# Seven block products for the branch gates of a hybrid layer, and merged sums kept raw until the last unit

## The chip, the cores and the metric

One core of one Trainium2 chip runs the whole network as one program. The metric is the device time of an execution in microseconds (us). TensorE (PE) multiplies matrices into PSUM banks; VectorE (DVE), ScalarE (ACT) and GpSimd (POOL) do the element-wise work; SyncE's queue (SP) issues the loads.

## The reference

A sequence of 512 tokens of width 1024 goes through an FFN, an attention mix, a second FFN, two hybrid layers and a last norm, all in float32. The change touches the end of a hybrid layer, where three branches `a`, `c`, `r` of width 512 are merged under gates that are three of the projections `h @ w_in`:

```python
def hybrid_layer(x, norm_g, w_in, ..., w_branch, w_out, layer):
    h = rms_norm(x, norm_g)
    proj = h @ w_in
    ...
    g = jax.nn.sigmoid(gates.astype(jnp.float32)).reshape(b, s, N_BRANCH, D_MODEL)
    branches = (a, c, r)
    merged = g[:, :, 0] * (branches[0] @ w_branch[0])
    for i in range(1, N_BRANCH):
        merged = merged + g[:, :, i] * (branches[i] @ w_branch[i])
    return x + (merged @ w_out).astype(x.dtype)
```

## The kernel before

**Products in two parts.** Each float32 operand is split into a high part (a rounded copy) and a low part (the rest), and a product is three matmuls, high by high, low by high, high by low (`three`, L1987 to L1989). Activations lie transposed in `xt_hi` and `xt_lo`, 8 blocks of 128 channels by 512 tokens. Weights come as slabs of 512 KB, 1024 float32 per partition: SP loads them in a fixed order into a ring of six slots (`load`, L512), ACT makes the high part (`highs`, L796), POOL the low part (`lows`, L665), PE uses the slab and gives the slot back (`w_used`). ACT casts `LEAD` = 4 slabs ahead of PE.

**The merge of a layer** is 12 units. Unit `nn` is branch `b = nn % 3` of the pair `jj = nn // 3` of output tiles (128 of the 1024 channels each), and takes three slabs: two of gate weights and one of branch weights. PE runs two gate tiles (`feature_tile`, 24 matmuls of 512 columns each) and the branch product (two times 12 of 512). ACT takes the sigmoid of each gate tile from its PSUM bank into `gate_sb` (L1224). DVE multiplies and adds, tile by tile:

```python
if b == 0:
    dve.tensor_tensor(m_sum[:, jh, :], src, g, ALU.mult)                  # L1957
else:
    dve.tensor_tensor(m_tmp[:, :], src, g, ALU.mult)                      # L1959
    ins = dve.tensor_tensor(m_sum[:, jh, :], m_sum[:, jh, :], m_tmp[:, :], ALU.add)   # L1961
```

After the third branch ACT makes the high part of the sum (L1280) and DVE the low (L1971). When all eight merged tiles stand, `out_product` multiplies them by `w_out`, eight more slabs of the same ring. Unit 2 also waits for `br_lo`, the low part of branch `r` (L1862).

**The FFN's seven products.** From its fourth unit on, an FFN takes its gate and up tiles (as one 2 by 2 block matrix) with the Strassen-Winograd scheme: seven products of half-size blocks instead of eight, each 12 matmuls of 256 columns (`product`, L2145 to L2147). That asks for sums of the activation blocks, made once (`x_sums`, their lows L1442), sums of the weight blocks per unit (DVE L1454, L1456, L1458 into PSUM, one by POOL, L729; their highs by ACT, lows by DVE L1463 and POOL L711), and combinations of the products on DVE (L1474 to L1516) and ACT (L938). The first three units run as plain tiles, with L1408 as their last step.

Every engine runs its own instructions in the order in which they are written, so what is queued behind a waiting instruction waits with it.

Of the kernel before, what the change touches and what calls it, by code (L numbers as in the profile page):

```python
# [8 lines left out]
ALU = mybir.AluOpType  # L9
# [6 lines left out]
P = 128  # L16
# [13 lines left out]
F0 = 3  # L30

# [101 lines left out]
def build(nc, x, ffn1_pre_g, ffn1_post_g, ffn1_w_gate, ffn1_w_up, ffn1_w_down, mix_pre_g, mix_post_g,  # L133
# [4 lines left out]
    with ExitStack() as ctx:  # L138
# [119 lines left out]
        m_hi_late = on("m_hi_late", [4, SEQ], 24, F32R)  # L258
# [6 lines left out]
        m_lo_late = on("m_lo_late", [4, SEQ], 48, F32R)  # L265
# [10 lines left out]
        m_lo_early = on("m_lo_early", [4, SEQ], 80, F32R)  # L276
# [92 lines left out]
        hhalf_done = sem("hhalf_done")  # L369
# [134 lines left out]
        def _(sp):  # L504
# [95 lines left out]
            for l in range(LAYERS):  # L600
# [25 lines left out]
                for jj in range(4):  # L626
# [7 lines left out]
                    if jj == 0:  # L634

                        sp.wait_ge(r_a_done, 16 * (l + 1))
                        gain(g_pre, norm_g_2[1:2, :] if l == 0 else final_norm_g_2.rearrange("(o d) -> o d", o=1),
                             pre_in)
                out_loads(s, w_out_2[l])
# [14 lines left out]
        def _(pool):  # L654
# [103 lines left out]
            for l in range(LAYERS):  # L758
# [11 lines left out]
                for h in range(4):  # L770
# [4 lines left out]
                    pool.tensor_tensor(sq_lo[:, :], r_sq[:, :], f32(sq_hi[:, :]), ALU.subtract).then_inc(rql_done, 1)  # L775
            lows(done, N_SLABS)
# [3 lines left out]
        def _(act):  # L780
# [10 lines left out]
            def highs(upto):  # L791

                for s in range(cast[0], min(upto, N_SLABS)):
# [3 lines left out]
                    cast[0] = s + 1  # L797

# [74 lines left out]
            def ffn(n):  # L873
# [18 lines left out]
                def x_sum_high(m):  # L892

                    act.wait_ge(xs_made, 4 * n + (1, 3, 3, 4)[m - 1])
                    act.activation(xs_hi[m][:, :, :], xs_raw[m][:, :, :], ACT.Copy).then_inc(xsh_done, 1)

# [18 lines left out]
                def up_high(s):  # L915

                    i = slot_of[s]
                    wait_raw(act, s)
                    act.activation(hi_slots[i][:, 512:SLAB], raw_slots[i][:, 512:SLAB], ACT.Copy).then_inc(hi_ready, 1)
                    cast[0] = s + 1  # L920

                highs(s0 + 2 * F0)
                gate(0)
                x_sum_high(1)
                x_sum_high(2)
                gate(1)
                x_sum_high(3)
                x_sum_high(4)
# [176 lines left out]
            for l in range(LAYERS):  # L1105
# [111 lines left out]
                def gate(nn, jh):  # L1217

                    n = 12 * l + nn
                    b4 = 4 if nn < 3 else 0  # L1220
# [46 lines left out]
                for nn in range(12):  # L1267
                    for jh in range(2):
                        highs(merge + 3 * nn + jh + 1 + LEAD)
# [5 lines left out]
                    highs(merge + 3 * nn + 3 + LEAD)  # L1275
                    if nn % 3 == 2:
                        for jh in range(2):
                            k = 2 * (nn // 3) + jh
                            act.wait_ge(ms_done, 8 * l + k + 1)
                            act.activation(m_hi(k), m_sum[:, jh, :], ACT.Copy).then_inc(mh_done, 1)  # L1280
# [5 lines left out]
        def _(dve):  # L1286
# [108 lines left out]

            def ffn(n):
# [13 lines left out]

                def quarter(k0, c0):

                    sl = slice(256 * c0, 256 * c0 + 256)
                    return f32(xt_hi[:, 4 * k0:4 * k0 + 4, sl]), f32(xt_lo[:, 4 * k0:4 * k0 + 4, sl])

                def whole(m, k0, c0):

                    hi, lo = quarter(k0, c0)
                    return dve.tensor_tensor(xs_part[m][:, :, :], hi, lo, ALU.add)  # L1419

                def x_sums():

                    dve.wait_ge(xtl_done, 8 * (2 * n + 1))
                    x11, x21, x22, x12 = (xs_part[m][:, :, :] for m in (2, 3, 1, 4))
                    s1, s2, s3, s4 = (xs_raw[m][:, :, :] for m in (1, 2, 3, 4))
                    whole(3, 0, 1)
                    link(whole(1, 1, 1))
                    dve.tensor_tensor(s1, x21, x22, ALU.add).then_inc(xs_made, 1)
                    link(whole(2, 0, 0))
                    dve.wait_ge(xs_made, 4 * n + 1)  # L1430
# [6 lines left out]
                def x_sum_low(m):  # L1437

                    dve.wait_ge(xsh_done, 4 * n + m)
                    if m < 4:  # L1440
                        dve.wait_ge(xs_made, 4 * n + 4)
# [1176 lines left out]
```

## Time and profile before

| what | value |
|---|---|
| median of 3 runs | 2048.14 us (2048.11 to 2048.17) |
| the profiled execution | 2048.16 us, span 2046.4 us |
| granted PE clock over the span | 1.00 |
| PE busy | 2028.4 us, 11280 matmuls |
| chain that ended last | PE 91%, DVE 6%, ACT 2% |
| the merge's PSUM sigmoids, L1224 | 48, mean 598 ns |
| slab loads | 3.4 to 3.9 us from issue to landing |

An engine's busy time counts instructions at work. A matmul's duration in the timeline is longer than the distance to the next one's start, because matmuls are pipelined: what a stretch of PE takes is read from starts.

### The profile page before, as it was taken

How to read it: one execution, taken by the hardware profiler on the slowest of the kernel's cores; microseconds unless marked ns; L12 is line 12 of the kernel's file. 1: busy time of each engine (PE TensorE's matmuls, PEld its weight loads, DVE VectorE, ACT ScalarE, POOL GpSimd, SP SyncE). 2: the span in 40 equal slices, each digit the busy share in tenths (PEclk: the TensorE clock that was granted, in tenths of full speed). 3: DMA queues.
4: the chain of work that ended last, by engine and by line, in shares of the span. 5: the costliest groups of instructions: out<-in, count | busy, mean ns of one | idle time of the engine just before them, and what ended most of it. 6: DMA issues, size and time to landing. Idle time of an engine off the chain costs nothing.

```text
span 2046.4 us, 28715 instructions
## 1 busy us (share of the span) xinstructions
PE 2028.4 (99%) x11280; PEld 1736.5 (85%) x11280; DVE 1110.8 (54%) x1822; ACT 910.1 (44%) x1657; POOL 994.3 (49%) x544
## 2 busy tenths in 40 slices
PE   9999999999999999999999999999999999999998
PEld 8999988877788999988888888888888888888887
DVE  7777720877848777802357674611133677562112
ACT  5445623467754444613444544322243544352222
POOL 4666644246654666643444343544434443364441
PEclk9999999999999999999999999999999999999999
DMA  6333332311133333333322222333333222233332
GB/s 190 99 105 109 104 97 93 122 42 32 32 113 104 104 104 105 102 103 114 108 74 75 73 80 82 103 100 96 93 129 93 72 73 79 76 103 94 94 102 72
DMA packets 244278, 191.53 MB, mean 94 GB/s; under 512 B 6448, under 2 KB 208816, under 8 KB 243760
## 3 DMA queue, kind: packets, MB, share of 16 engines
q1 hardware_dynamic: 244144, 189.70, 30.7%
q8 instruction: 90, 1.47, 0.3%
q14 instruction: 44, 0.36, 0.1%
HBM read 187.58 MB, written 2.10 MB: 93 GB/s over the span
## 4 chain that ended last, share of the span: by engine, by line
PE 91%; DVE 6%; ACT 2%; issue 1%; SPq 0%; DMA 0%; POOL 0%; DVEq 0%; ACTq 0%
PE bank L1987 22%; PE bank L1989 21%; PE bank L1988 21%; PE bank L2145 6%; PE bank L2146 6%; PE bank L2147 6%; PE bank L1981 3%; PE bank L2278 1%; PE bank L2446 1%; PE bank L2298 1%; DVE xs_lo L1442 1%; PE bank L2305 1%; DVE xs_part L1419 1%; DVE xn L1304 0%; DVE x_tok L1309 0%
## 5 line engine op out<-in xcount | busy, mean ns | idle before, releaser
L665 POOL TENSOR_TENSOR w_lo<-w_raw,w_hi 128x1024 fp32r<-128x1024 f32 x248 | 612.8, 2478 | 610.9 <-ACT w_hi L796 609.9
L796 ACT ACTIVATE w_hi<-w_raw 128x1024 fp32r<-128x1024 f32 x287 | 300.8, 1054 | 227.7 <-DMA w_raw<-in_ffn_w_down 125.6
L1987 PE MATMUL bank<-xt_hi,w_hi 128*128 128x512 f32 (+1 forms) x896 | 343.0, 383 | 0.5
L1988 PE MATMUL bank<-xt_lo,w_hi 128*128 128x512 f32 (+1 forms) x896 | 338.9, 378 | 0.0
L1989 PE MATMUL bank<-xt_hi,w_lo 128*128 128x512 f32 (+1 forms) x896 | 338.9, 378 | 0.0
L1987 PEld LDWEIGHTS bank<-xt_hi,w_hi 128*128 128x128 f32 x896 | 168.5, 188 | 39.3 <-issue 6.7
L1989 PEld LDWEIGHTS bank<-xt_hi,w_lo 128*128 128x128 f32 x896 | 168.6, 188 | 32.0
L1988 PEld LDWEIGHTS bank<-xt_lo,w_hi 128*128 128x128 f32 x896 | 168.7, 188 | 29.7
L1987 PE MATMUL bank<-w_hi,xt_hi 128*128 128x512 f32 (+1 forms) x456 | 178.2, 391 | 0.0
L1989 PE MATMUL bank<-w_hi,xt_lo 128*128 128x512 f32 (+1 forms) x456 | 174.4, 383 | 0.0
L1988 PE MATMUL bank<-w_lo,xt_hi 128*128 128x512 f32 (+1 forms) x456 | 174.3, 382 | 0.0
L1987 PE MATMUL bank<-w_hi,h_hi 128*128 128x512 f32 x352 | 137.1, 390 | 0.0
L1988 PE MATMUL bank<-w_lo,h_hi 128*128 128x512 f32 x352 | 137.0, 389 | 0.0
L1989 PE MATMUL bank<-w_hi,h_lo 128*128 128x512 f32 x352 | 136.9, 389 | 0.0
L2145 PE MATMUL bank<-xs_hi,ws_hi 128*128 128x256 f32 x456 | 129.3, 283 | 0.0
L2146 PE MATMUL bank<-xs_lo,ws_hi 128*128 128x256 f32 x456 | 129.0, 283 | 0.0
L2147 PE MATMUL bank<-xs_hi,ws_lo 128*128 128x256 f32 x456 | 129.0, 283 | 0.0
L1959 DVE TENSOR_TENSOR m_tmp<-bank,gate_sb 128x512 f32<-128x512 f32 x32 | 22.1, 692 | 180.2 <-PE bank L1989 179.6
L734 POOL TENSOR_TENSOR w_lo<-w_raw,w_hi 128x1024 fp32r<-128x1024 f32 x38 | 91.8, 2415 | 30.6 <-ACT w_hi L796 19.1
L1224 ACT ACTIVATE gate_sb<-bank 128x512 f32<-128x512 f32 x48 | 28.5, 598 | 173.6 <-PE bank L1989 173.6
L1298 DVE RECIPROCAL stat<-stat 128x1 f32<-128x1 f32 x12 | 2.0, 163 | 190.1 <-ACT stat L808 190.1
L1987 PEld LDWEIGHTS bank<-w_hi,xt_hi 128*128 128x128 f32 x456 | 85.7, 188 | 20.2 <-issue 3.0
(358 smaller groups left out, 4874.2 us busy)
## 6 DMA issues: line engine op xcount, KB each, us to landing
w_raw<-in_w_in SPq DMA_DIRECT2D x132, 512.0 KB, 3.8
w_raw<-in_ffn_w_down SPq DMA_DIRECT2D x44, 512.0 KB, 3.6
w_raw<-in_ffn_w_gate SPq DMA_DIRECT2D x43, 512.0 KB, 3.8
w_raw<-in_ffn_w_up SPq DMA_DIRECT2D x43, 512.0 KB, 3.9
w_raw<-in_w_out SPq DMA_DIRECT2D x24, 512.0 KB, 3.7
w_raw<-in_w_branch SPq DMA_DIRECT2D x24, 512.0 KB, 3.4
w_raw<-in_w_qkv SPq DMA_DIRECT2D x16, 512.0 KB, 3.9
x_tok<-in_x SPq DMA_DIRECT2D x4, 512.0 KB, 7.0
```

Source lines behind the costliest of these rows:

```text
L665: pool.tensor_tensor(lo_slots[i], raw_slots[i], f32(hi_slots[i]), ALU.subtract).then_inc(lo_ready, 1)
L734: pool.tensor_tensor(lo_slots[i], raw_slots[i], f32(hi_slots[i]), ALU.subtract).then_inc(lo_ready, 1)
L796: act.activation(hi_slots[i], raw_slots[i], ACT.Copy).then_inc(hi_ready, 1)
L1224: act.activation(gate_sb[:, jh, :], bank[b4 + jh][:, :], ACT.Sigmoid).then_inc(gs_done, 1)
L1959: dve.tensor_tensor(m_tmp[:, :], src, g, ALU.mult).then_inc(gm_done, 1)
L1981: ins = pe.matmul(dst[:, cols(k)], blk, ident[:, :], is_transpose=True)
L1987: pe.matmul(out_ap, ah, bh, start=first, stop=False)
L1988: pe.matmul(out_ap, ah, bl, start=False, stop=False)
L1989: return pe.matmul(out_ap, al, bh, start=False, stop=last)
L2145: pe.matmul(dst, wh, xh, start=k == 0 and not onto, stop=False, skip_group_check=onto)
L2146: pe.matmul(dst, wh, xl, start=False, stop=False, skip_group_check=onto)
L2147: ins = pe.matmul(dst, wl, xh, start=False, stop=k == 3, skip_group_check=onto)
```

## The change

Units 4 to 11 of both layers (`M0` = 4) no longer compute their two gate tiles with 48 matmuls of 512 columns, but with seven products of 12 matmuls of 256 columns, in the order P1, P6, P4, P2, P7, P5, P3, in banks `g_x`, `g_y`, `g_v`, `g_z`, `g_w`. The activation sums (`ms_*`) are made on DVE and ACT during units 2 to 4 of each layer. The weight sums S3, S2 and S4 (DVE) lie in the PSUM banks of the branch products (`p_a`, `p_b`) and in `g_t`; sum 1 is made by POOL (`t_raw1`, L831, and its low, L842). Combinations v1 (ACT, L1385), v2 and v3 (DVE) give four quarter tiles, with a sigmoid of 256 columns each. The merged sums stay raw in SBUF (`m_raw`), the product with the gate stays in PSUM, and the splits into `m_hi` and `m_lo` come in unit 11. The load of the next norm's gain moves from behind the first pair's slabs to behind the fifth `w_out` slab. Core of the diff:

```diff
+M0 = 4
...
                 out_loads(s, w_out_2[l], next_gain)
...
+                def next_gain():
+                    sp.wait_ge(prod_done, gate_product(l, 11, 4))
+                    gain(g_pre, ..., pre_in)
...
+                for nn in range(M0, 12):                                   # POOL
+                    q, g = before_gate(l, nn), merge_start(l) + 3 * nn
+                    if nn > M0:
+                        lows(g - 1, g)
+                        pool.wait_ge(ws1l_done, q)
+                    pool.tensor_tensor(t_raw1[:, :], raw_slots[j][:, 0:512], raw_slots[i][:, 0:512], ALU.subtract)
+                    pool.wait_ge(ws_made, 3 * q + 3)
+                    pool.tensor_tensor(lo_slots[i], raw_slots[i], f32(hi_slots[i]), ALU.subtract).then_inc(lo_ready, 1)
+                    pool.tensor_tensor(lo_slots[j][:, 512:SLAB], raw_slots[j][:, 512:SLAB], ...)
+                    pool.tensor_tensor(lo, pairs(t_raw1[:, :]), f32(hi), ALU.subtract).then_inc(ws1l_done, 1)
...
+                for nn in range(M0, 12):                                   # ACT
+                    act.activation(v1[:, :], g_x, ACT.Copy).then_inc(u1_done, 1)
+                    highs(g + 3)
+                    if nn < 11:
+                        gate_sum_high(nn + 1, 2)
+                        gate_sum_high(nn + 1, 4)
+                    sigmoid(0, 0, g_x)
+                    if nn < 11:
+                        highs(g + 4)
+                        up_high(g + 4)
+                    else:
+                        for k in range(4):
+                            merged_high(k)
+                    sigmoid(0, 1, g_v)
+                    if nn < 11:
+                        gate_sum_high(nn + 1, 3)
+                        gate_sum_high(nn + 1, 1)
+                    sigmoid(1, 1, g_z)
+                    act.wait_ge(uplo_done, q + 1)
+                    sigmoid(1, 0, g_w)
+                merged_high(4)
+                merged_high(5)
+                highs(merge + N_MERGE + 2)
...
+                        dve.tensor_tensor(src, src, g, ALU.mult).then_inc(gm_done, 1)          # merged, L2089
+                        dve.tensor_tensor(m_raw[k][:, :], src, m_raw[k][:, :], ALU.add)        # L2092
...
+                def gate_w_sums(nn):
+                    dve.tensor_tensor(g_sum[3], w2[:, 512:SLAB], w2[:, 0:512], ALU.subtract)   # L2111
+                    dve.tensor_tensor(g_sum[2], g_sum[3], w1[:, 0:512], ALU.add)               # L2113
+                    dve.tensor_tensor(g_sum[4], g_sum[2], w1[:, 512:SLAB], ALU.subtract)       # L2115
...
+                    merged(nn)                                             # DVE, unit M0 - 1
+                gate_sum_low(M0, 4)
+                x_sum_low(2 + l, 1, 3, ms_hi, ms_lo, ms_raw)
+                gate_sum_low(M0, 3)
+                x_sum_low(2 + l, 4, 4, ms_hi, ms_lo, ms_raw)
+                for nn in range(M0, 12):                                   # DVE
+                    if nn < 11:
+                        gate_w_sums(nn + 1)
+                    dve.tensor_tensor(v2[:, :], g_y, v1[:, :], ALU.add).then_inc(u2_done, 1)   # L2155
+                    if nn < 11:
+                        gate_sum_low(nn + 1, 2)                                                # L2122
+                        gate_sum_low(nn + 1, 4)
+                    dve.tensor_tensor(v3[:, :], g_y, v1[:, :], ALU.add).then_inc(u3_done, 1)
+                    dve.tensor_tensor(g_v, v3[:, :], g_v, ALU.subtract).then_inc(gsum_done, 1)
+                    dve.wait_ge(prod_done, gate_product(l, nn, 5))
+                    dve.tensor_tensor(v2[:, :], g_z, v2[:, :], ALU.add).then_inc(upart_done, 1)  # L2168
+                    dve.tensor_tensor(g_z, g_z, v3[:, :], ALU.add).then_inc(uphi_done, 1)        # L2170
+                    if nn < 11:
+                        gate_sum_low(nn + 1, 3)
+                    else:
+                        for k in range(4):
+                            merged_low(k)
+                    dve.tensor_tensor(g_w, g_w, v2[:, :], ALU.add).then_inc(uplo_done, 1)        # L2178
+                    if nn == 11:
+                        merged_low(4)
+                        merged_low(5)
+                    merged(nn)
...
+                    pe.wait_ge(u2_done, q + 1)                             # PE: P7, then P5, P3
+                    product(g_y, gate_w_sum(3, s), m_sum(3), onto=True).then_inc(prod_done, 1)
+                    pe.wait_ge(ws1l_done, q + 1)
+                    for jh in range(2):
+                        wait_merged(pe, l, nn - 1, jh)
+                    pe.wait_ge(gs_done, gate_count(l, nn - 1, 1) - 1)
+                    product(g_z, gate_w_sum(1, s), m_sum(1)).then_inc(prod_done, 1)
+                    ready(s + 1)
+                    product(g_w, w_quarter(s + 1, 1), m_sum(4)).then_inc(w_used, 1)
+                    if nn < 11:
+                        pe.wait_ge(wsl_done, 3 * q + 6)
+                    branch_product(nn, (p_a, p_b))
```

How the order of instructions moves is shown at three places. First DVE's queue in a late unit of the first layer's merge, before: the end of a unit with `b` = 2 and what follows (`m_tmp`, `m_sum` in SBUF, `bank` is a PSUM bank).

```order
L1959 TENSOR_TENSOR m_tmp<-bank,gate_sb 128x512 [waits gs_done,ms_done]
L1961 TENSOR_TENSOR m_sum<-m_sum,m_tmp 128x512 [waits gm_done]
L1971 TENSOR_TENSOR m_lo_late<-m_sum,m_hi_late 128x512 [waits mh_done,ms_done]
L1971 TENSOR_TENSOR m_lo_late<-m_sum,m_hi_late 128x512 [waits mh_done]
L1957 TENSOR_TENSOR m_sum<-bank,gate_sb 128x512 [waits mh_done,ml_done,gs_done,w_used]
L1957 TENSOR_TENSOR m_sum<-bank,gate_sb 128x512 [waits ml_done,mh_done,gs_done]
L1959 TENSOR_TENSOR m_tmp<-bank,gate_sb 128x512 [waits gs_done,w_used]
L1961 TENSOR_TENSOR m_sum<-m_sum,m_tmp 128x512 [waits gm_done]
```

And with the change, from P5's combinations in unit 4 over its merge to v2 of unit 5 (`v_184` is v2, `v_185` is v3, `xt_lo` of 128x2x256 is a weight sum's low; the banks of L2111 to L2115 are the weight sums):

```order
L2168 TENSOR_TENSOR v_184<-bank,v_184 128x256 [waits u2_done,prod_done]
L2170 TENSOR_TENSOR bank<-bank,v_185 128x256 [waits upart_done]
L2122 TENSOR_TENSOR xt_lo<-bank,xt_hi 128x2x256 [waits wsh_done]
L2178 TENSOR_TENSOR bank<-bank,v_184 128x256 [waits upart_done,w_used]
L2089 TENSOR_TENSOR bank<-bank,gate_sb 128x512 [waits gs_done,w_used]
L2092 TENSOR_TENSOR m_raw_196<-bank,m_raw_196 128x512 [waits gm_done]
L2089 TENSOR_TENSOR bank<-bank,gate_sb 128x512 [waits gs_done]
L2092 TENSOR_TENSOR m_raw_197<-bank,m_raw_197 128x512 [waits gm_done]
L2111 TENSOR_TENSOR bank<-w_raw 128x512 [waits ma_done,wsl_done,raw_in3,raw_in2]
L2113 TENSOR_TENSOR bank<-bank,w_raw 128x512 [waits ws_made]
L2115 TENSOR_TENSOR bank<-bank,w_raw 128x512 [waits ws_made]
L2155 TENSOR_TENSOR v_184<-bank,v_183 128x256 [waits uplo_done,u1_done,prod_done]
```

The multiply and add stand there as before, the add with a PSUM operand; ahead of them stand the combinations and the low of S3, behind them the weight sums of the next unit, and v2 behind those.

Second, DVE's queue at the entry, from the low of S2 for unit 4 over the merge of unit 3 to v2 of unit 4 (`t_lo` is the low of S4, `ms_lo_84` and `ms_lo_83` are the lows of the activation sums s1 and s4). Before, two multiplies of unit 3 stood there alone.

```order
L2122 TENSOR_TENSOR xt_lo<-bank,xt_hi 128x2x256 [waits wsh_done]
L2087 TENSOR_TENSOR m_raw_196<-bank,gate_sb 128x512 [waits gs_done,w_used]
L2087 TENSOR_TENSOR m_raw_197<-bank,gate_sb 128x512 [waits gs_done]
L2122 TENSOR_TENSOR t_lo<-bank,t_hi 128x512 [waits wsh_done]
L1563 TENSOR_TENSOR ms_lo_84<-ms_raw_92,ms_hi_80 128x1024 [waits xs_made,xsh_done]
L2122 TENSOR_TENSOR xt_lo<-bank,xt_hi 128x2x256 [waits wsh_done]
L1563 TENSOR_TENSOR ms_lo_83<-ms_raw_91,ms_hi_79 128x1024 [waits xsh_done]
L2111 TENSOR_TENSOR bank<-w_raw 128x512 [waits gm_done,wsl_done,raw_in4,raw_in1]
L2113 TENSOR_TENSOR bank<-bank,w_raw 128x512 [waits ws_made]
L2115 TENSOR_TENSOR bank<-bank,w_raw 128x512 [waits ws_made]
L2155 TENSOR_TENSOR v_184<-bank,v_183 128x256 [waits uplo_done,u1_done,prod_done]
```

Five operations of preparation and the three sums for unit 5 stand between the merge of unit 3 and v2.

Third, ACT's queue at the exit of the first layer's merge, before: the sigmoids of unit 11, between them casts of `w_out` slabs (`w_hi`).

```order
L1224 ACTIVATE gate_sb<-bank 128x512 [waits gm_done,w_used]
L796 ACTIVATE w_hi<-w_raw 128x1024 [waits raw_in0]
L1224 ACTIVATE gate_sb<-bank 128x512 [waits gm_done,w_used]
L796 ACTIVATE w_hi<-w_raw 128x1024 [waits raw_in1]
L1280 ACTIVATE m_hi_late<-m_sum 128x512 [waits ms_done] x2
L796 ACTIVATE w_hi<-w_raw 128x1024 [waits raw_in4]
L796 ACTIVATE w_hi<-w_raw 128x1024 [waits raw_in5]
```

And with the change, from v1 of unit 11 on (`m_hi_210` to `m_hi_215` are merged highs, the cast behind v1 is that of the last branch slab):

```order
L864 ACTIVATE w_hi<-w_raw 128x1024 [waits raw_in5]
L1351 ACTIVATE gate_sb<-bank 128x256 [waits gm_done,w_used]
L1357 ACTIVATE m_hi_210<-m_raw_194 128x512 [waits ms_done,prod_done]
L1357 ACTIVATE m_hi_211<-m_raw_195 128x512 [waits ms_done,prod_done]
L1357 ACTIVATE m_hi_212<-m_raw_196 128x512 [waits ms_done,prod_done]
L1357 ACTIVATE m_hi_213<-m_raw_197 128x512 [waits ms_done,prod_done]
L1351 ACTIVATE gate_sb<-bank 128x256 [waits gsum_done]
L1351 ACTIVATE gate_sb<-bank 128x256 [waits gm_done,uphi_done]
L1351 ACTIVATE gate_sb<-bank 128x256 [waits uplo_done]
L1357 ACTIVATE m_hi_214<-m_raw_198 128x512 [waits ms_done,prod_done]
L1357 ACTIVATE m_hi_215<-m_raw_199 128x512 [waits ms_done,prod_done]
L864 ACTIVATE w_hi<-w_raw 128x1024 [waits raw_in2]
```

The first cast of a `w_out` slab now stands behind the fourth sigmoid and six merged highs.

## Rows read from the trace of the kernel before

Times in a timeline are us from the span's start; after the engine come the line, the operation, out<-in, and in brackets the idle time before it and what ended that.

**Rows 1.** Page, part 1: busy us, share of the span, instructions.
```profile
PE 2028.4 (99%) x11280; PEld 1736.5 (85%) x11280; DVE 1110.8 (54%) x1822; ACT 910.1 (44%) x1657; POOL 994.3 (49%) x544
```

**Rows 2.** Timeline, PE, first merge, unit 0 to 1: start us, duration us, operation.
```profile
1285.79 0.39 PE L1987 MATMUL bank<-xt_hi,w_hi 128*128 128x512 f32 x1
...
1291.23 0.39 PE L1987 MATMUL bank<-c_hi,w_hi 128*128 128x512 f32 x1
```

**Rows 3.** Timeline, PE, two units of the second FFN.
```profile
705.73 0.28 PE L2145 MATMUL bank<-xt_hi,w_hi 128*128 128x256 f32 x1
...
715.81 0.28 PE L2145 MATMUL bank<-xt_hi,w_hi 128*128 128x256 f32 x1
```

**Rows 4.** Waits of PE: us in total, times, longest us.
```profile
PE bank L2145 <- DVE h_raw L1408: 3.3, 2, 1.7
```

**Rows 5.** Timeline, PE and ACT, the branch product of unit 2.
```profile
1307.32 0.39 PE L1989 MATMUL bank<-xt_hi,w_lo 128*128 128x512 f32 x1
...
1307.75 0.60 ACT L1224 ACTIVATE gate_sb<-bank 128x512 f32<-128x512 f32 x1 [3.89 <-PE bank L1989]
...
1307.86 0.50 PE L1987 MATMUL bank<-br_hi,w_hi 128*128 128x512 f32 x1
...
1308.19 0.39 PE L1988 MATMUL bank<-br_lo,w_hi 128*128 128x512 f32 x1
```

**Rows 6.** Timeline, POOL and DVE, the merge of unit 1.
```profile
1297.32 2.40 POOL L665 TENSOR_TENSOR w_lo<-w_raw,w_hi 128x1024 fp32r<-128x1024 f32 x1 [7.10 <-ACT w_hi L796]
...
1297.65 2.62 DVE L1961 TENSOR_TENSOR m_sum<-m_sum,m_tmp 128x512 f32<-128x512 f32 x1
...
1303.11 4.70 DVE L1862 TENSOR_TENSOR br_lo<-r_out,br_hi 128x512 fp32r<-128x512 f32 x4
```

**Rows 7.** Timeline, DVE, the same two FFN units.
```profile
703.92 0.68 DVE L1463 TENSOR_TENSOR ws_lo<-bank,ws_hi 128x512 fp32r<-128x512 f32 x1
704.52 0.41 DVE L1474 TENSOR_TENSOR up_hi<-bank,u 128x256 f32<-128x256 f32 x1
704.85 0.41 DVE L1479 TENSOR_TENSOR u<-bank,u 128x256 f32<-128x256 f32 x1
...
705.51 0.69 DVE L1454 TENSOR_TENSOR bank<-w_raw 128x512 f32<-128x512 f32 x1
706.24 0.70 DVE L1456 TENSOR_TENSOR bank<-bank,w_raw 128x512 f32<-128x512 f32 x1
...
715.59 1.60 DVE L1454 TENSOR_TENSOR bank<-w_raw 128x512 f32<-128x512 f32 x1
```

**Rows 8.** One line, the FFN's activation-sum lows: ns min/median/max.
```profile
L1442 DVE TENSOR_TENSOR xs_lo<-xs_raw,xs_hi x8: 1214/2310/2346, 40.1 to 653.7; 128x1024 fp32r<-128x1024 f32 x8
```

**Rows 9.** Timeline, ACT and POOL, the first slab of `w_out`, layer 0.
```profile
1442.55 1.06 ACT L796 ACTIVATE w_hi<-w_raw 128x1024 fp32r<-128x1024 f32 x1 [2.24 <-DMA w_raw<-in_w_out]
...
1443.69 2.40 POOL L665 TENSOR_TENSOR w_lo<-w_raw,w_hi 128x1024 fp32r<-128x1024 f32 x1 [0.91 <-ACT w_hi L796]
```

**Rows 10.** Timeline, ACT, an FFN unit: a 256-column copy, then a cast.
```profile
707.37 0.38 ACT L938 ACTIVATE u<-bank 128x256 f32<-128x256 f32 x1 [1.91 <-PE bank L2147]
707.65 1.06 ACT L796 ACTIVATE w_hi<-w_raw 128x1024 fp32r<-128x1024 f32 x1
```

**Rows 11.** Timeline, POOL, the same FFN units.
```profile
705.54 1.81 POOL L711 TENSOR_TENSOR ws_lo<-ws_raw,ws_hi 128x512 fp32r<-128x512 f32 x1 [3.08 <-ACT ws_hi L908]
...
715.34 1.29 POOL L711 TENSOR_TENSOR ws_lo<-ws_raw,ws_hi 128x512 fp32r<-128x512 f32 x1 [2.79 <-ACT ws_hi L908]
```

**Rows 12.** Timeline, POOL and DVE starting close together in the mix, layer 0.
```profile
1192.73 2.42 POOL L665 TENSOR_TENSOR w_lo<-w_raw,w_hi 128x1024 fp32r<-128x1024 f32 x1 [4.46 <-ACT w_hi L796]
1198.36 2.96 POOL L665 TENSOR_TENSOR w_lo<-w_raw,w_hi 128x1024 fp32r<-128x1024 f32 x1 [3.21 <-ACT w_hi L796]
...
1192.81 2.88 DVE L1927 TENSOR_TENSOR o<-o,stat 128x512 f32<-128x512 f32 x1
...
1198.38 0.68 DVE L1927 TENSOR_TENSOR o<-o,stat 128x512 f32<-128x512 f32 x1
```

More of the change, by code:

```diff
@@ L797, in highs, with x_sum_high, up_high @@
                     cast[0] = s + 1
+            def x_sum_high(n, m, hi, raw):
+                act.wait_ge(xs_made, 4 * n + (1, 3, 3, 4)[m - 1])
+                act.activation(hi[m][:, :, :], raw[m][:, :, :], ACT.Copy).then_inc(xsh_done, 1)
+            def up_high(s):
+                i = slot_of[s]
+                wait_raw(act, s)
+                act.activation(hi_slots[i][:, 512:SLAB], raw_slots[i][:, 512:SLAB], ACT.Copy).then_inc(hi_ready, 1)
+                cast[0] = s + 1
             def norm_f(b, c):
@@ L1265, in _, with gate_sum_high, sigmoid, merged_high @@
                 out_root(3)
-                for nn in range(12):
+                def gate_sum_high(nn, m):
+                    q = before_gate(l, nn)
+                    if m == 1:
+                        act.wait_ge(ws1_made, q + 1)
+                        src, done = t_raw1[:, :], ws1h_done
+                    else:
+                        act.wait_ge(ws_made, 3 * q + 3)
+                        src, done = g_sum[m], wsh_done
+                        if nn > M0:
+                            act.wait_ge(prod_done, gate_product(l, nn - 1, {2: 6, 3: 7, 4: 4}[m]))
+                        else:
+                            act.wait_ge(w_used, merge + 3 * nn - 1)
+                    act.activation(gate_sum_tiles(m, merge + 3 * nn)[0], pairs(src), ACT.Copy).then_inc(done, 1)
+                def sigmoid(jh, half, src):
+                    act.activation(gate_sb[:, jh, cols(half, 256)], src, ACT.Sigmoid).then_inc(gs_done, 1)
+                def merged_high(k):
+                    act.wait_ge(prod_done, gate_product(l, 11, 6 if k < 4 else 7))
+                    act.wait_ge(ms_done, 8 * l + k + 1)
+                    act.activation(m_hi[k][:, :], m_raw[k][:, :], ACT.Copy).then_inc(mh_done, 1)
+                top = merge + 3 * M0
+                for nn in range(M0):
                     for jh in range(2):
-                        highs(merge + 3 * nn + jh + 1 + LEAD)
+                        highs(min(merge + 3 * nn + jh + 1 + LEAD, top))
                         if nn > 0:
@@ L1274, in _ @@
                                 retained_high(h)
[L1275 to L1280, printed above, removed]
+                    highs(min(merge + 3 * nn + 3 + LEAD, top))
+                    if nn == M0 - 2:
+                        for m in (2, 3, 1):
+                            x_sum_high(2 + l, m, ms_hi, ms_raw)
@@ L2100, in out_product, with x_quarter, x_sum, w_quarter @@
                         turn_chunk(b, c - 2)
+            def x_quarter(k0, c0):
+                sl = slice(256 * c0, 256 * c0 + 256)
+                return lambda k: (xt_hi[:, 4 * k0 + k, sl], xt_lo[:, 4 * k0 + k, sl])
+            def x_sum(m, hi=xs_hi, lo=xs_lo):
+                return lambda k: (hi[m][:, k, :], lo[m][:, k, :])
+            def w_quarter(s, k0):
+                return lambda k: slab(s, 4 * k0 + k, KD, P)
+            def w_sum(m):
+                return lambda k: (ws_hi[m][:, k, :], ws_lo[m][:, k, :])
+            def product(dst, w, x, onto=False):
+                for k in range(4):
+                    (wh, wl), (xh, xl) = w(k), x(k)
+                    pe.matmul(dst, wh, xh, start=k == 0 and not onto, stop=False, skip_group_check=onto)
+                    pe.matmul(dst, wh, xl, start=False, stop=False, skip_group_check=onto)
+                    ins = pe.matmul(dst, wl, xh, start=False, stop=k == 3, skip_group_check=onto)
+                return ins
             def ffn(n):
```

362 lines of the change are left out of this document (236 added, 126 removed).

## The prediction

> **What bounds the kernel now.** I read the busy times first: TensorE (PE) works 99% of the span, VectorE (DVE), GpSimd (POOL) and ScalarE (ACT) about half of it [rows 1]. So the time is PE's, and the others count only where PE waits for them. Then PE's timeline in the merge, where the change is: a gate tile's first matmul starts at 1285.79, the next product's first at 1291.23. These are 24 matmuls of 512 columns in 5.44 us, 226.7 ns each, with nothing between them [rows 2]. Then a place where the seven-product scheme already runs: in the second FFN a unit's first matmul starts at 705.73, the next unit's at 715.81, 84 matmuls of 256 columns at 120 ns [rows 3]. Then PE's list of waits: the product line of the FFN waits twice in all, once per FFN, 3.3 us, for an operation of DVE (L1408) that only the units ahead of the scheme have: at its entry [rows 4]. Everything else in those units is covered. The question is whether the merge's units are covered as well.
>
> The profiled execution took 2048.16 us (span 2046.4), the median of the runs is 2048.14: one base for the sum. A measurement of this kernel tells a change from none from about 0.2% on, 4.1 us.
>
> **What it takes off PE.** Sixteen units lose two gate tiles (2 x 5.44 = 10.88 us) and get 84 matmuls of 256 columns (84 x 0.12 = 10.08): 0.80 each, **12.8 us**. The branch product stays. Besides, unit 2 loses a wait. Its branch product starts at 1307.86 instead of 1307.55 and its second matmul follows after 0.33 instead of 0.227, so it is 0.31 + 0.10 late [rows 5]; that 0.10 comes after a PE wait, and I add it to each below. It waited for `br_lo`, which DVE ended at 1307.81, and DVE was late by an add with two SBUF operands that took 2.62 us because POOL had begun a subtraction 0.33 us before [rows 6]. The new add L2092 takes one operand from PSUM, and 1.9 us less suffice: **0.8 us** in two layers.
>
> **What it adds, where PE can wait.** Steps, all from rows: a 256-column matmul's results reach DVE or ACT 0.28 + 0.04 after its start, a 512-column one's 0.39 + 0.04, DVE's reach PE after 0.05 [rows 3, 5, 6]. On DVE, 256 columns take 0.41, 0.33 from start to start; 512 columns 0.68, 0.60 from start to start, 0.73 where the next needs the result [rows 7].
>
> *Before the branch product, units 4 to 10, both layers (14 times).* PE now waits for the low of S3 for the next unit (L2122), since the branch product overwrites the bank that holds S3. In DVE's queue that low stands behind L2168 and L2170, which need P5. From the start of P5's last matmul: 0.32, then 0.45 (L2170 needs L2168), 0.33, 0.68, 0.05 = 1.83 us. PE is there after P3, 13 x 0.12 = 1.56. Late by 0.27 + 0.10: **5.2 us**. No lock is in play, S3 lies in PSUM.
>
> *Entry, unit 4 (twice).* P7 waits for v2 (L2155). Count from the start of the previous branch product's last matmul. PE reaches P7 at 0.23 + 48 x 0.12 = 5.99. DVE starts at 0.43 and has, in order: two multiplies L2087 (1.20), T4's low (0.60), the low of s1 (1.21, the shortest of the same operation in the FFN [rows 8]), S3's low (0.60), the low of s4 (1.21), the next unit's weight sums (0.73 + 0.73 + 0.61), v2 0.41, 0.05: 7.78. That is 1.79 late at best. But s4's low (two SBUF operands) comes up at 4.04, and POOL has the low of unit 4's branch slab from 3.28 (worked out below) for 2.40, to 5.68: 1.64 more. POOL's next, the raw sum 1 (1.30), then stands ready when s4's low ends, with L2111 behind it: some 1.1 more. The FFN's entry has such a row, a median of 2.31 against 1.21 [rows 8]. I take both collisions, 4.5 + 0.10 each: **9.2 us**, the ends 3.8 and 9.7.
>
> *Exit, unit 11 (twice).* Before, ACT cast four slabs ahead, the first of `w_out` at 1442.55, and POOL began its low at 1443.69, while the last unit's gate tiles had yet to run [rows 9]. Now the casts stand in ACT's queue behind the last sigmoid and two merged highs. From the first matmul of the last branch product: L2168 at -1.24, L2170 at -0.79, four merged lows from -0.46 (4 x 0.60), L2178 at 1.94, the sigmoid 0.46 later at 2.40, two highs from 2.68 (an estimate of half the 1.05 of a 1024-column cast, 0.52 each), the slab's cast at 3.72, its low at 3.72 + 1.05 + 0.08 = 4.85 [rows 9, 10], done at 7.25, PE at 7.30. The branch product ends at 5.44: 1.86 + 0.10 late, **3.9 us**. Later slabs come 2.4 us apart on POOL and PE needs 5.44 for each.
>
> *P5 waits on three semaphores,* every other product on one or two, and no row shows three. Below: nothing, since the FFN's waits vanish in the 120 ns. Above: a PE wait's 0.10 twice. I take 0.10, in the middle: **1.6 us** over 16, ends 0 and 3.2.
>
> *At nothing:* the slabs and bytes are the same. ACT's added highs and POOL's sum 1 fit: per unit of 15.5 us POOL has two lows of 2.40 and three operations of 1.30, 8.7 us [rows 9, 11]. DVE's first activation sums stand in unit 2 ahead of adds that PE needs 11 us later. The gain load on SP's queue waits for P4 of unit 11, which is earlier than P3, for which the slab ahead of it waits anyhow; the gain is read after eight `w_out` slabs of 5.44 us.
>
> **Sum:** -12.8 - 0.8 + 5.2 + 9.2 + 3.9 + 1.6 = +6.3, so 2048.16 + 6.3 = **2054.5**.
>
> **What is a toss-up.** In iterations 5, 6, 8 and 9 of each layer (8 times) DVE and POOL reach for the lock at nearly one time. From the last matmul of the branch product before: DVE merges (0.43 + 0.73 + 0.60 + 0.73 + 0.73 = 3.22) and comes to L2111, whose operands both lie in SBUF. Its further waits may cost 0.08. POOL comes to the branch slab's low after P1 (0.23 + 11 x 0.12 + 0.32), ACT's v1 (0.28) and cast (1.05 + 0.08): 3.28 [rows 9, 10]. So DVE is between 0.06 before and 0.02 after POOL. Where DVE started 0.03 ahead in the FFN it took 0.69 and POOL waited; where POOL was 0.25 ahead, DVE took 1.60 [rows 7, 11]. In the mix stage a DVE start 0.02 after POOL's took 0.68 and POOL 2.96; 0.08 after POOL's it took 2.88 [rows 12]. So I give DVE the better chance. If DVE goes first, v2 is done at 3.30 + 0.73 + 0.73 + 0.61 + 0.46 = 5.83, in time for 5.99.
>
> **Rivals.**
> *B, POOL first.* L2111 starts at 5.70, v2 reaches PE at 5.70 + 2.07 + 0.46 = 8.23: 2.24 + 0.10 late, 8 times, +18.7: 2073.2. For it: the 0.02 at DVE's worst end. Against: the row in which DVE won from there. By the Trainium skill, "SBUF — State Buffer", section "SBUF: two separate sides", the port pair is an exclusive lock, and whichever operation starts first has it for the whole instruction; strictly read, with DVE's waits counted, that is this rival. The trace agrees on the lock and the whole instruction, and within 0.02 us not on who wins.
> *C, some of the eight,* since the two starts drift by what a stall adds: 2057 to 2071.
> *D, entry without collisions* (POOL's low later than s4's low, the sum later than L2111), or with one, and P5 for nothing: up to 5.4 and 1.6 less, 2047.5 to 2052. For it: 0.76 us decide. Against: the FFN's entry collides.
> *E, faster:* matmuls of 256 columns come closer than 120 ns here. 16 x 84 = 1344 of them; at half of 226.7 the time is 8.9 us less (2045.6), at 112 ns or below it is under 2044. Against: the FFN's 120 holds over whole units. The Trainium skill, "TensorE: Matmul & The Clock Gate", section "Wait — 56ns, not 53.3ns?", gives N / 2.4 GHz + 2.5 ns at full clock, 109 and 215.7 ns. The rows show 120 and 226.7, so its rule is not met here; with its 109 alone the time would be 2039.7.
>
> **Numbers.** My forecast 0.42 (2052 to 2057), B 0.29, C 0.10, D 0.13, E 0.06. Faster is E, the same is D, slower the rest: 0.06, 0.13, 0.81. The forecast's own range is 2052 to 2057; 8 in 10 need D and B as well: 2047 to 2074, leaving out E and the far ends of B.
>
> **What would show it.** Right: seven-product units at 10.08 us plus about 0.1 at P5; a gap of 0.27 before branch products of units 4 to 10 for DVE's L2122; 4.5 us before P7 of unit 4, released by L2155; 1.9 us before the first `w_out` product, released by POOL. B shows as L2111 at 2.4 to 3.1 us instead of 0.69 with PE waiting 2.2 us before P7. Wrong: no wait at the branch product (then S3's low is done earlier than I follow), an entry under 2 us, or a spacing other than 120 ns.

## The result and the profile after

The changed kernel takes 2081.11 us (median of 4 runs, 2079.17 to 2081.58), the kernel before 2048.12 on the same chip: ratio 1.016, interval 1.0147 to 1.0172, 33 us slower. The forecast was 6.3 us slower, 2054.5, and the range of 2047 to 2074 does not hold the time.

First the page's part 1 and the granted clock of the changed kernel's profiled execution (2081.58 us), which answer to [rows 1].

```profile
PE 2032.8 (98%) x11856; PEld 1765.6 (85%) x11856; DVE 1260.8 (61%) x2038; ACT 951.9 (46%) x1777; POOL 1023.8 (49%) x576
...
core 0: 2079.8 us, clock 0.993
```

PE's busy time, in which the ends of matmuls are modelled, grew by 4.4 us, though by the spacing of the starts PE has 12.8 us less to do, and the clock of the whole span is 0.993, where it was 1.00. DVE has 150 us more, and is still busy for only 61% of the span. So the loss is in waits and in the clock. The waits of PE (us in total, times, longest), which answer to [rows 4]:

```profile
PE bank L2332 <- DVE v L2155: 24.1, 10, 4.4
PE bank L2199 <- POOL w_lo L708: 3.5, 2, 1.8
PE bank L2332 <- DVE h_raw L1577: 3.3, 2, 1.7
```

The FFN's entry is what it was (now L1577). New are ten waits for v2 (L2155), 24.1 us, and two for POOL's low of a slab (L708), 3.5 us. PE's timeline in unit 5 of the first layer shows the wait ahead of P7, the start of P5, and the start of the branch product, with the operation of DVE that the branch product waits for:

```profile
1357.64 0.28 PE L2334 MATMUL bank<-xt_hi,w_lo 128*128 128x256 f32 x1
1359.85 0.39 PE L2332 MATMUL bank<-ms_hi,xt_hi 128*128 128x256 f32 x1 [1.93 <-DVE v L2155]
...
1361.26 0.28 PE L2334 MATMUL bank<-ms_hi,xt_lo 128*128 128x256 f32 x1
1361.38 0.28 PE L2332 MATMUL bank<-ms_hi,w_hi 128*128 128x256 f32 x1
...
1364.14 0.28 PE L2334 MATMUL bank<-ms_hi,w_lo 128*128 128x256 f32 x1
1364.56 0.50 PE L2199 MATMUL bank<-br_hi,w_hi 128*128 128x512 f32 x1
1364.90 0.39 PE L2200 MATMUL bank<-br_lo,w_hi 128*128 128x512 f32 x1
...
1363.83 0.68 DVE L2122 TENSOR_TENSOR xt_lo<-bank,xt_hi 128x512 fp32r<-128x512 f32 x1
```

PE is idle for 1.93 us ahead of P7; counted by starts, as below, P7 comes 2.20 us after the matmul before it instead of 0.12, so it is 2.08 late. P5 (1361.38) follows the last matmul of P7 after 0.12 us: its three semaphores cost nothing. The branch product (1364.56) starts 0.30 late, 0.05 after DVE has ended the low of S3 (L2122), and its second matmul follows after 0.34 instead of 0.227, the same pair of losses as in [rows 5]. In the same unit, DVE's first merge multiply (L2089), POOL's low and DVE's first weight sum for the next unit, which answer to [rows 12]:

```profile
1355.05 2.40 POOL L708 TENSOR_TENSOR w_lo<-w_raw,w_hi 128x1024 fp32r<-128x1024 f32 x1 [8.60 <-ACT w_hi L864]
...
1352.21 0.70 DVE L2089 TENSOR_TENSOR bank<-bank,gate_sb 128x512 f32<-128x512 f32 x1 [5.48 <-PE bank L2201]
...
1355.10 2.90 DVE L2111 TENSOR_TENSOR bank<-w_raw 128x512 f32<-128x512 f32 x1
```

POOL starts 0.05 us ahead of DVE, takes 2.40, and L2111 takes 2.90 instead of 0.69. All eight places read alike: POOL 0.04 to 0.05 ahead, L2111 at 2.90 or 2.91. At the entry of the first layer, POOL, DVE and PE's P7:

```profile
1332.22 2.63 POOL L708 TENSOR_TENSOR w_lo<-w_raw,w_hi 128x1024 fp32r<-128x1024 f32 x1 [0.73 <-ACT w_hi L864]
1334.79 2.26 POOL L831 TENSOR_TENSOR t_raw<-w_raw 128x512 f32<-128x512 f32 x1
...
1333.10 2.83 DVE L1563 TENSOR_TENSOR ms_lo<-ms_raw,ms_hi 128x1024 fp32r<-128x1024 f32 x1
1335.85 1.75 DVE L2111 TENSOR_TENSOR bank<-w_raw 128x512 f32<-128x512 f32 x1
...
1338.98 0.41 DVE L2155 TENSOR_TENSOR v<-bank,v 128x256 f32<-128x256 f32 x1
...
1339.45 0.58 PE L2332 MATMUL bank<-ms_hi,xt_hi 128*128 128x256 f32 x1 [4.36 <-DVE v L2155]
```

The low of s4 (1333.10) takes 2.83 behind the branch slab's low, sum 1 (1334.79) waits for it, L2111 takes 1.75 behind sum 1, and PE idles 4.36 us for v2 (1338.98), 4.52 by starts. At the exit, ACT, POOL and PE's first output product:

```profile
1464.10 2.18 ACT L1357 ACTIVATE m_hi<-m_raw 128x512 fp32r<-128x512 f32 x4
...
1470.36 0.39 ACT L1351 ACTIVATE gate_sb<-bank 128x256 f32<-128x256 f32 x1 [2.35 <-DVE bank L2178]
...
1471.69 2.00 ACT L864 ACTIVATE w_hi<-w_raw 128x1024 fp32r<-128x1024 f32 x2
...
1472.82 4.73 POOL L708 TENSOR_TENSOR w_lo<-w_raw,w_hi 128x1024 fp32r<-128x1024 f32 x2 [9.50 <-ACT w_hi L864]
...
1475.33 0.47 PE L2199 MATMUL bank<-w_hi,m_hi 128*128 128x512 f32 x1 [1.76 <-POOL w_lo L708]
```

Four merged highs, the last sigmoid (1470.36, released by L2178), two more highs, then the two casts, and POOL's low from 1472.82: the first output product starts 1.92 us late by starts (PE is idle for 1.76 of it).

The clock is a part of its own. Three stretches of the first layer. Each line has the stretch, its length, and the busy time (and instructions) of PE, PEld, DVE, ACT and POOL; then come the granted clock, the DMA share and GB/s.

```profile
1350.00:1375.00 25.00, 22.94 (x159) 21.21 (x158) 15.75 (x21) 7.63 (x14) 10.78 (x6) 1.00 0.29 85
1375.00:1390.00 15.00, 12.93 (x72) 11.56 (x72) 6.87 (x13) 4.98 (x10) 7.12 (x5) 0.89 0.25 71
1390.00:1405.00 15.00, 14.86 (x105) 13.83 (x104) 7.74 (x14) 6.52 (x12) 8.55 (x5) 1.00 0.35 105
```

And in the middle one PE's timeline behind a wait:

```profile
1377.97 0.39 PE L2332 MATMUL bank<-ms_hi,xt_hi 128*128 128x256 f32 x1 [1.92 <-DVE v L2155]
1378.19 0.28 PE L2333 MATMUL bank<-ms_lo,xt_hi 128*128 128x256 f32 x1
1378.32 0.28 PE L2334 MATMUL bank<-ms_hi,xt_lo 128*128 128x256 f32 x1
...
1379.04 0.42 PE L2333 MATMUL bank<-ms_lo,xt_hi 128*128 128x256 f32 x1
1379.26 0.41 PE L2334 MATMUL bank<-ms_hi,xt_lo 128*128 128x256 f32 x1
```

After a wait of 1.92 us the matmuls of 256 columns start 0.12 us apart at first (1378.19, 1378.32), and then 0.21: the lower of TensorE's two clock levels, 1.2 GHz instead of 2.4. Such a stretch stands behind both waits of 4.4 us at the entries and behind five of the eight of 1.9 us (none behind that of 1359.85). By the Trainium skill, "TensorE: Matmul & The Clock Gate", section "What's actually happening", the gate passes half or all of the clock, by how busy PE has lately been. The spacings of 0.12 and 0.21 agree with two levels and no third.

Counted from the starts of PE's matmuls in both merges, everything beyond the regular spacing: entry 2 x 4.52 = 9.0, ahead of P7 8 x 2.085 = 16.7, ahead of branch products and behind their first matmul 5.2, exit 4.0, 256-column matmuls further apart 11.9 (126 of them: 118 at the lower clock make 11.1, and eight are the 0.10 behind a wait for v2). Together 46.8, less 12.8 and 0.8: 33.2, of the measured 33.4 between the two profiled executions.

### The profile page after: what moved, and what is told of

Its sections match the earlier page's. It is cut to its first block and busy times, and to the rows that moved or that the text cites. A ratio compares the mean times of both kernels' runs of the same rounds, so it can differ in the third digit from the quotient of the medians.

```text
span 2079.8 us, 30543 instructions
## 1 busy us (share of the span) xinstructions
PE 2032.8 (98%) x11856; PEld 1765.6 (85%) x11856; DVE 1260.8 (61%) x2038; ACT 951.9 (46%) x1777; POOL 1023.8 (49%) x576
## 5 line engine op out<-in xcount | busy, mean ns | idle before, releaser
L708 POOL TENSOR_TENSOR w_lo<-w_raw,w_hi 128x1024 fp32r<-128x1024 f32 x216 | 537.2, 2497 | 543.8 <-ACT w_hi L864 543.5
L2199 PE MATMUL bank<-xt_hi,w_hi 128*128 128x512 f32 (+1 forms) x640 | 243.4, 380 | 0.5
L2200 PE MATMUL bank<-xt_lo,w_hi 128*128 128x512 f32 (+1 forms) x640 | 239.3, 374 | 0.0
L2201 PE MATMUL bank<-xt_hi,w_lo 128*128 128x512 f32 (+1 forms) x640 | 239.3, 374 | 0.0
L2199 PEld LDWEIGHTS bank<-xt_hi,w_hi 128*128 128x128 f32 x640 | 120.5, 188 | 29.3 <-issue 6.7
L2201 PEld LDWEIGHTS bank<-xt_hi,w_lo 128*128 128x128 f32 x640 | 120.5, 188 | 22.0
L2200 PEld LDWEIGHTS bank<-xt_lo,w_hi 128*128 128x128 f32 x640 | 120.6, 189 | 19.7
L2333 PE MATMUL bank<-xt_lo,w_hi 128*128 128x256 f32 x432 | 122.2, 283 | 0.0
L2334 PE MATMUL bank<-xt_hi,w_lo 128*128 128x256 f32 x432 | 122.2, 283 | 0.0
L2332 PE MATMUL bank<-xt_hi,w_hi 128*128 128x256 f32 x432 | 122.2, 283 | 0.0
L777 POOL TENSOR_TENSOR w_lo<-w_raw,w_hi 128x1024 fp32r<-128x1024 f32 x38 | 91.8, 2415 | 30.5 <-ACT w_hi L864 19.1
```

Source lines behind the costliest of these rows:

```text
L708: pool.tensor_tensor(lo_slots[i], raw_slots[i], f32(hi_slots[i]), ALU.subtract).then_inc(lo_ready, 1)
L777: pool.tensor_tensor(lo_slots[i], raw_slots[i], f32(hi_slots[i]), ALU.subtract).then_inc(lo_ready, 1)
L2199: pe.matmul(out_ap, ah, bh, start=first, stop=False)
L2200: pe.matmul(out_ap, ah, bl, start=False, stop=False)
L2201: return pe.matmul(out_ap, al, bh, start=False, stop=last)
L2332: pe.matmul(dst, wh, xh, start=k == 0 and not onto, stop=False, skip_group_check=onto)
```

## Experiments

All times are medians; in brackets stand the ratio to the kernel before and its 95% interval. The kernel before stood at 2047.99 beside the runs with v1 copied twice, with waits put into the kernel before, and with all mended, at 2047.87 beside the other four.

**The lock, with POOL made to wait.**

```diff
                     if nn > M0:
+                        if nn > M0 + 1:
+                            pool.wait_ge(ws_made, 3 * q + 1)
                         lows(g - 1, g)
```

> Edit: from unit 6 on, POOL's low of the branch slab also waits for the first weight sum (L2111) of the next unit, so DVE has the lock first. Theory (lock): PE's eight waits of 2.08 us ahead of P7, released by v2, are there because POOL began its low 0.05 us before L2111; with DVE first L2111 takes 0.69, the eight waits go (8 x 2.19 = 17.5 us with the 0.10 behind each), and so do the stretches at 213 ns behind them, about 85 of 122 matmuls at 0.093 us each (7.9): 2055.7 us, granted clock about 0.998, PE's wait list left with two entries of 4.4 us and two of 1.8. Rival (queue): v2 is late because DVE's queue is too long in itself, whoever has the lock; then PE still waits about 2 us for v2 and the time stays within 3 us of 2081. Rival (products slow the clock): the waits go, but the 213 ns stretches stay because the 256-column products themselves bring them: about 2063.6.

Measured 2057.74 (1.0048, interval 1.0033 to 1.0063), clock 0.997. The first weight sum (now L2113: ns min/median/max over all 16) and PE's waits:

```profile
L2113 DVE TENSOR_TENSOR bank<-w_raw x16: 693/700/1754, 1322.2 to 1974.4; 128x512 f32<-128x512 f32 x16
...
PE bank L2334 <- DVE v L2157: 8.7, 2, 4.4
PE bank L2201 <- POOL w_lo L708: 3.5, 2, 1.8
```

The sum's median is 700 ns and its longest 1754, where eight of the sixteen took 2.90 us in the changed kernel, and of PE's long new waits only those at the two entries and exits are left. The matmuls at the lower clock fell from 118 to 42 with the eight waits, all of them behind the entries, so neither the queue rival nor the one by which the products themselves slow the clock holds.

**The entry.** The wait on POOL for unit 4 as well (`nn > M0`).

> Edit: as the run before, and for the branch slab of unit 4 too, so that at the entry POOL's low and its sum 1 come behind L2111 of unit 5. Theory (lock, two collisions at the entry): the wait ahead of P7 of unit 4 falls from 4.5 to 1.8 us in both layers (-5.4) and, without waits above 2 us, the last 213 ns stretches (about 37 matmuls, 3.5 us) go too: 2046.8 us. Rival (queue): the wait at the entry stays 4.5 since DVE's list of eleven operations is what counts: no change against the run before, 2055.7.

Measured 2048.66 (1.0004, interval 0.9995 to 1.0013), 9.1 below the run before. PE's waits for v2 and the clock:

```profile
PE bank L2334 <- DVE v L2157: 3.3, 2, 1.7
...
core 0: 2046.4 us, clock 0.999
```

The entry's wait falls from 4.4 to 1.7 us, and with it the last stretches at the lower clock; one matmul in each layer, the one behind the wait, is still late. So the list of operations ahead of v2 costs 1.8 us, and the two collisions with POOL 2.7, as the forecast had them. Without the lock and the clock the change neither gains nor loses: 3.9 at the entry, 4.0 at the exit and, by this run's own starts, 5.7 at the branch products (all fourteen at 0.30 + 0.11) take the whole of the 13.6.

**The lock, with POOL late by itself.** The same without a new wait on POOL: ACT copies v1 twice in units 5 to 10, and waits only for its own first copy.

```diff
+                    if M0 < nn < 11:
+                        act.activation(v1[:, :], g_x, ACT.Copy).then_inc(act_step, 1)
+                        steps[0] += 1
+                        act.wait_ge(act_step, steps[0])
                     act.activation(v1[:, :], g_x, ACT.Copy).then_inc(u1_done, 1)
```

> Edit: in units 5 to 10 ACT copies v1 twice, the second over the first, so that the cast behind it and POOL's low of the branch slab come about 0.3 to 0.4 us later; nothing waits differently. Theory (the lock goes to whoever starts first, and 0.05 us decide): POOL now comes after L2111, which takes 0.69, the eight waits of 2.08 us go without any new wait on POOL: as with the wait on POOL, 2057.7 us, within 1 us. Rival (the wait on POOL did something else, such as letting the weight sums run undisturbed): L2111 still takes 2.9 in most units, 2075 to 2081.

Measured 2057.64. DVE's sum and POOL's low in unit 5 (L2115 is the sum, L708 the low):

```profile
1354.56 0.70 DVE L2115 TENSOR_TENSOR bank<-w_raw 128x512 f32<-128x512 f32 x1
...
1354.92 2.60 POOL L708 TENSOR_TENSOR w_lo<-w_raw,w_hi 128x1024 fp32r<-128x1024 f32 x1 [8.28 <-ACT w_hi L864]
```

DVE comes first by 0.36 us and takes 0.70; POOL takes 2.60, 0.2 more than when it comes first. At the other seven places DVE is 0.36 or 0.37 ahead and takes 0.70 as well. An added copy of 0.38 us on a third engine makes the kernel 23 us faster. What decides is who starts first.

**The branch product's wait.** The low of S3 ahead of the two combinations that need P5.

```diff
+                    if nn < 11:
+                        gate_sum_low(nn + 1, 3)
                     dve.wait_ge(prod_done, gate_product(l, nn, 5))
...
                     dve.tensor_tensor(g_z, g_z, v3[:, :], ALU.add).then_inc(uphi_done, 1)
-                    if nn < 11:
-                        gate_sum_low(nn + 1, 3)
-                    else:
+                    if nn == 11:
                         for k in range(4):
                             merged_low(k)
```

> Edit: only the low of S3 for the next unit is moved ahead of the two combinations that need P5 on DVE. Theory: the 14 waits of 0.30 + 0.10 us ahead of the branch products go, 5.6 us: 2075.5, if the eight waits and the stretches at 213 ns stay as they are (these may shift by 2 us). Rival: the low is late because ACT's high of S3 is late, not because of its place on DVE: no change, 2081.

Measured 2074.47 (2073.79 to 2077.08), 6.6 less. In PE's timeline no branch product of units 4 to 10 is late any more, and the waits for v2 are unchanged (24.2 us). Its place on DVE was the cause. The wait can make 5.2 of the 6.6; between the two profiled executions the time fell by 4.5. The rest lies within the spread of the single runs.

**The exit.** The first output slab is cast ahead of the merged highs.

```diff
                     else:
+                        highs(merge + N_MERGE + 1)
                         for k in range(4):
                             merged_high(k)
```

> Edit: only ACT's cast of the first output slab is moved ahead of the first four merged highs, behind the first sigmoid of unit 11, so that POOL can make its low during the last branch product. Theory: the two waits of 1.9 us ahead of the first output product go, 4.0 us: 2077.1. Rival: POOL's low then collides with the merged lows on DVE and the first output product waits for those instead: within 1 us of 2081.

Measured 2079.01, with single runs from 2073.9 to 2080.7. The wait for POOL's low (3.5 us) is gone from PE's list and nothing has taken its place. But the time fell by 2.1 only, and by 0.9 between the two profiled executions: here 158 matmuls are further apart, not 126, some 3 us more, which takes back most of the 4.0 that the two waits were worth. The mechanism is shown by the list, its size by PE's starts. The medians cannot show it, since what stands at the lower clock varies by as much from run to run.

**The clock, without the 256-column products.** The kernel before, with PE made to wait in units 5, 6, 8 and 9 for multiplies whose results nothing reads.

```diff
+                    if nn + 1 in (5, 6, 8, 9):
+                        for _ in range(4 if b == 1 else 5):
+                            link(dve.tensor_tensor(m_tmp[:, :], bank[b4 + 3][:, :], gate_sb[:, 1, :], ALU.mult))
+                        dve.wait_ge(dve_step, steps[0])
+                        dve.tensor_tensor(m_tmp[:, :], ...).then_inc(pad_done, 1)
...
+                        if jh == 1 and nn in (5, 6, 8, 9):
+                            pe.wait_ge(pad_done, ...)
                         feature_tile(s + jh, bank[b4 + jh][:, :])
```

> Edit: the kernel before, with PE made to wait in units 5, 6, 8 and 9 of both layers ahead of the second gate tile, for a row of five or six multiplies of DVE whose results nothing reads: eight waits of 2.1 to 2.5 us among 512-column matmuls, 19 us in all. Theory (the waits bring the clock down): stretches of matmuls at half clock behind most of them, about 1.1 us each as in the changed kernel: 2076 us, granted clock below 0.997. Rival (it takes the 256-column products): no such stretch, 2067 us, clock 1.000.

Measured 2078.72, 30.7 above the kernel before. DVE's last added multiply (L1972) and PE behind it at the second wait (512 columns), two stretches of the first layer (one without a wait, one with), and the clock of the span:

```profile
1371.73 0.69 DVE L1972 TENSOR_TENSOR m_tmp<-bank,gate_sb 128x512 f32<-128x512 f32 x1
...
1372.52 0.76 PE L1993 MATMUL bank<-xt_hi,w_hi 128*128 128x512 f32 x1 [1.99 <-issue]
1373.08 0.63 PE L1994 MATMUL bank<-xt_lo,w_hi 128*128 128x512 f32 x1
1373.51 0.63 PE L1995 MATMUL bank<-xt_hi,w_lo 128*128 128x512 f32 x1
...
1376.26 0.40 PE L1993 MATMUL bank<-xt_hi,w_hi 128*128 128x512 f32 x1
1376.49 0.39 PE L1994 MATMUL bank<-xt_lo,w_hi 128*128 128x512 f32 x1
...
1330.00:1350.00 20.00, 20.00 (x90) 16.57 (x89) 4.87 (x6) 4.16 (x5) 8.97 (x4) 1.00 0.35 106
1370.00:1390.00 20.00, 18.01 (x73) 14.47 (x72) 6.81 (x8) 4.15 (x5) 9.23 (x4) 0.91 0.27 79
...
core 0: 2077.0 us, clock 0.994
```

PE starts 0.10 us after DVE has ended, so the wait is the added one, though the profile names no releaser. After a wait of 1.99 us the starts are 0.43 apart and from 1376.26 again 0.23. Such a stretch stands behind seven of the eight waits. By starts the waits make 18.5 of the 30.7 us, the matmuls further apart some 10. So waits of 2 us bring the clock down with 512-column matmuls too; the products of 256 columns are not needed for it.

**All mended.** The three edits above, and at the entry v2 ahead of the low of s4 and of the sums for unit 5, with the low and high of S3 for unit 5 ahead of what follows P7.

```diff
+                        if nn > M0:
+                            pool.wait_ge(ws_made, 3 * q + 1)
...
                 gate_sum_low(M0, 4)
-                x_sum_low(2 + l, 1, 3, ms_hi, ms_lo, ms_raw)
                 gate_sum_low(M0, 3)
-                x_sum_low(2 + l, 4, 4, ms_hi, ms_lo, ms_raw)
+                x_sum_low(2 + l, 1, 3, ms_hi, ms_lo, ms_raw)
...
+                    if nn == M0:
...
+                        dve.tensor_tensor(v2[:, :], g_y, v1[:, :], ALU.add).then_inc(u2_done, 1)
+                        x_sum_low(2 + l, 4, 4, ms_hi, ms_lo, ms_raw)
                     if nn < 11:
                         gate_w_sums(nn + 1)
...
+                    if nn == M0:
+                        gate_sum_low(nn + 1, 3)          # DVE, ahead of v3; ACT's high of it ahead of highs(g + 4)
...
```

> Edits together: the wait on POOL for unit 4 and later, the low of S3 ahead of the combinations of P5, the cast of the first output slab ahead of the merged highs, and at the entry v2, the low and the high of S3 ahead of what P7 does not need. Theory: all waits named are the whole loss, so the 12.8 + 0.8 us stay: 2035 us, granted clock 1.000, no wait of DVE's v or of POOL's low in PE's list. Rival (a further wait comes up behind those removed, at the entry or in POOL's late low of the branch slab): 2038 to 2044.

Measured 2035.97 (2035.94 to 2036.2): ratio 0.9941 to the kernel before, interval 0.9927 to 0.9956. Page, waits and clock:

```profile
PE 2015.7 (99%) x11856; PEld 1753.7 (86%) x11856; DVE 1236.7 (61%) x2038; ACT 951.0 (47%) x1777; POOL 1017.8 (50%) x576
...
PE bank L2346 <- DVE h_raw L1583: 3.3, 2, 1.7
PE bank L2207 <- DVE xn L1478: 2.5, 6, 0.6
...
core 0: 2033.7 us, clock 1.000
```

PE's longest waits are the FFN's and the norms' again, and in each merge half a microsecond is left, 0.08 behind the first matmul of each of the seven branch products. The seven products are worth what their count and spacing say, once nothing waits: 2047.99 - 13.6 = 2034.4, measured 1.6 above.

## Why the prediction was wrong

Between the two profiled executions the change cost 33.4 us, where the sum had 6.3. The 27 us between them are 17.5 of the lock, which the forecast gave to DVE, and 11.1 of the clock, which no term had, less the 1.6 of P5 that did not come. By the prediction's own steps:

- *Off PE, 12.8 + 0.8.* Right. The spacing stays 0.12 outside the stretches at the lower clock, and the mended kernel shows the gain. Rival E falls with it.
- *Before the branch product, 5.2.* Right in its mechanism: L2122 of DVE releases it, and moving that low took the wait away. Its size was a little short: 0.30 + 0.11 each instead of 0.27 + 0.10, 5.7 for fourteen, as the run with POOL held back at the entry shows. That the changed kernel's trace has 5.2 too is luck, since one of its fourteen waits vanishes and another is halved, both in units whose matmuls ran at the lower clock.
- *Entry, 9.2.* Right: 9.0, with both collisions; the run with POOL held back leaves the 1.8 that was worked out for the list alone. Rival D falls.
- *Exit, 3.9.* Right: 4.0.
- *P5's three semaphores, 1.6.* Too much: nothing, the lower of the two ends. Waits that are satisfied when PE comes to them cost nothing here, as in the FFN.
- *The toss-up.* **This step failed.** It put DVE between 0.06 us before and 0.02 after POOL and gave DVE the better chance (0.42 against 0.29 for rival B), by a row in which DVE had won from 0.02 behind [rows 12]. DVE came 0.05 behind, each time, and lost, each time. From the merge's first multiply to L2111 it needs 2.89 us, as 1352.21 to 1355.10 shows, not the 2.79 of my terms: a further wait of L2111 costs 0.10 where I had 0.08 as the far end. Rival B had the right mechanism and the right price, 16.7 for eight waits and 0.8 behind them against 18.7. The two ways differ by 17.5 us, and the sum of a dozen rounded terms cannot place 0.05 us. An even chance would have been the most that the rows bear out. Nor were there eight tosses: counted from the start of the last matmul of the branch product before (1351.78 at the place shown), POOL starts at 3.27 and L2111 at 3.32 at every one of the eight, so nothing drifts, and rival C falls.
- *The clock.* **No case had it.** The sum put a wait at its own length and at nothing for the matmuls behind it. B's 2073 was nearly the top of the range; the measured time is 8 us above it, and 11.1 us of the loss are matmuls at the lower clock. The kernel before showed a granted clock of 1.00, but its PE waited for 1.7 us at most, and only twice. The price of a 2 us wait that comes again is not the wait alone: here it was nearly another half of it (11.1 on 25.7), among 512-column matmuls a little over half (10 on 18.5).

By the Trainium skill, "SBUF — State Buffer", section "SBUF: two separate sides", whoever starts first has the port pair for the whole instruction. The trace agrees, at 0.05 us and for 2.40 us, and so do both runs that let DVE start first. I weighed one row at 0.02 us against it; at 0.05 the rule was the better guide. Why DVE won from 0.02 behind in that row stays open, since no run here came as close.

## What to carry to other kernels

When two engines reach for one lock within a tenth of a microsecond of each other, do not forecast the winner: price both ways, and write an order (a semaphore, or an operation moved) that settles it, because 0.05 us decided 23 us here. Here a saving of 0.8 us a unit showed only once the operations that PE waits for stood ahead of those that it does not wait for; four small edits of the order turned +33 us into -12. And where a PE wait of 2 us recurs, allow up to half as much again, since the clock may drop behind it.

## What was not expected of the hardware

PE waits of 1.9 us and more that recur every 18 to 37 us brought the granted clock to about 0.9 in stretches of 15 to 20 us, with starts at 0.21 instead of 0.12 us (256 columns) and at 0.43 instead of 0.227 (512 columns). It follows most such waits: in the changed kernel both of 4.4 us (these alone, too, once the eight were gone) and 5 of 8 of 1.9 us, in the kernel before with waits put in 7 of 8 of 2.0 to 2.4 us. With the first output slab cast early it followed 7 of the 8 of 1.9 us, so it differs from run to run, by several microseconds of time. Behind the waits of 1.7 to 1.8 us (the FFN's, the exit's, and the entry's with POOL held back) none of the profiled executions shows it. Which of the longer waits are followed by it stays open.
